# First stage with single k-steps between modulation pieces, and a projection with its short chunks between the long ones

## What is computed

```python
mod_x = silu(c) @ w_ada + b_ada          # 2048 -> 6 x 2048, also for c_ctx
sh1, s1, g1, sh2, s2, g2 = split(mod_x, 6)
h  = rmsnorm(x, norm1_w) * (1 + s1) + sh1     # and hc from ctx with the context's sh1, s1
p  = h @ w_in                                 # q, k, v | c_q (384) | c_kv (256) | k_rope (64)
q_mla = rmsnorm(c_q) @ w_uq
kv    = rmsnorm(c_kv) @ w_ukv
```

## Time and profile before

| | |
|---|---|
| median of 3 runs | 3177.64 us (3173.39 to 3178.29) |
| profiled execution | 3180.76 us, span 3178.9 us |
| PE busy | 2911.0 us, 92% of the span |
| DVE busy | 1804.0 us, 57% |
| ACT busy | 1191.1 us, 37% |
| mean granted TensorE clock | 0.96 of 2.4 GHz |

### The profile page before, as it was taken

How to read it: one execution, slowest core, us unless ns; L and a number is a source line. 1 busy time by engine, 2 the same in 40 slices (tenths; PEclk the granted TensorE clock), 3 DMA queues, 4 the chain that set the end, 5 groups by cost and what they waited for, 6 DMA issues and landing times.

```text
span 3178.9 us, 35028 instructions
## 1 busy us (share of the span) xinstructions
PE 2911.0 (92%) x13848; PEld 2378.0 (75%) x13848; DVE 1804.0 (57%) x2015; ACT 1191.1 (37%) x1134; POOL 165.0 (5%) x338
## 2 busy tenths in 40 slices
PE   5888895778999999999799999998879899999997
PEld 2587673467888888888587888887768788888886
DVE  1385776664555645555455557984754544555553
ACT  2232213433444434344344434333333343444332
POOL 0000005200000000000000100015300000000000
PEclk8999897999999999999889999999989999999999
DMA  8687875535456565546354876665236456555554
GB/s 333 245 293 259 304 255 185 179 132 192 164 172 206 174 210 186 184 162 206 96 199 169 269 224 215 223 201 167 60 120 207 150 164 207 199 189 193 169 174 134
DMA packets 347323, 617.34 MB, mean 194 GB/s; under 512 B 51232, under 2 KB 102064, under 8 KB 339776
## 3 DMA queue, kind: packets, MB, share of 16 engines
q1 hardware_dynamic: 310320, 582.69, 55.2%
q10 hardware_dynamic: 36880, 32.94, 3.1%
HBM read 586.57 MB, written 29.00 MB: 194 GB/s over the span
## 4 chain that ended last, share of the span: by engine, by line
PE 79%; DVE 11%; DMA 4%; ACT 3%; issue 2%; SPq 0%; POOL 0%; ACTq 0%; DVEq 0%; POOLq 0%
PE ps L306 21%; PE ps L307 21%; PE ps L308 21%; DVE w_lo L269 3%; PE ps L974 2%; PE ps L975 2%; PE ps L976 2%; DMA raw<-in_pack_ada 1%; DVE upd L2155 1%; PE ps L1199 1%; PE ps L587 1%; DVE w_lo L754 1%; DMA proj_q<-stg 1%; PE ps L2453 1%; PE ps L385 1%
## 5 line engine op out<-in xcount | busy, mean ns | idle before, releaser
L269 DVE TENSOR_TENSOR w_lo<-raw,w_hi 128x2048 fp32r<-128x2048 f32 (+3 forms) x428 | 892.0, 2094 | 703.7 <-ACT w_hi L262 702.4
L262 ACT ACTIVATE w_hi<-raw 128x2048 fp32r<-128x2048 f32 (+3 forms) x428 | 745.1, 1753 | 785.1 <-PE ps L308 728.0
L306 PE MATMUL ps<-w_hi,a_hi 128*128 128x512 f32 (+1 forms) x2272 | 892.2, 393 | 17.2 <-DVE a_lo L626 7.0
L308 PE MATMUL ps<-w_hi,a_lo 128*128 128x512 f32 (+1 forms) x2272 | 885.9, 390 | 0.0
L307 PE MATMUL ps<-w_lo,a_hi 128*128 128x512 f32 (+1 forms) x2272 | 885.6, 390 | 0.0
L306 PEld LDWEIGHTS ps<-w_hi,a_hi 128*128 128x128 f32 x2272 | 431.1, 190 | 109.8 <-DVE a_lo L626 8.7
L308 PEld LDWEIGHTS ps<-w_hi,a_lo 128*128 128x128 f32 x2272 | 430.8, 190 | 88.8
L307 PEld LDWEIGHTS ps<-w_lo,a_hi 128*128 128x128 f32 x2272 | 431.0, 190 | 85.6
L306 PE MATMUL ps<-w_hi,b_hi 128*128 128x512 f32 x864 | 339.0, 392 | 10.6 <-DVE w_lo L269 5.7
L308 PE MATMUL ps<-w_hi,b_lo 128*128 128x512 f32 x864 | 337.5, 391 | 0.0
L307 PE MATMUL ps<-w_lo,b_hi 128*128 128x512 f32 x864 | 337.4, 391 | 0.0
(11 more groups left out here) (319 smaller groups left out, 2788.3 us busy)
## 6 DMA issues: line engine op xcount, KB each, us to landing
raw<-in_hyb_w_in SPq DMA_DIRECT2D x96, 1024.0 KB, 5.3
raw<-in_sc_w_in SPq DMA_DIRECT2D x96, 1024.0 KB, 5.1
raw<-in_w_up SPq DMA_DIRECT2D x88, 1024.0 KB, 5.0
raw<-in_pack_ada SPq DMA_DIRECT2D x96, 512.0 KB, 6.2
raw<-in_w_down SPq DMA_DIRECT2D x48, 768.0 KB, 4.4
raw<-in_w_in SPq DMA_DIRECT2D x24, 1024.0 KB, 7.3
raw<-in_hyb_w_out SPq DMA_DIRECT2D x32, 768.0 KB, 4.5
raw<-in_sc_w_out SPq DMA_DIRECT2D x32, 768.0 KB, 4.4
```

The lines of the kernel that those rows point to most:

```text
L262: nc.scalar.activation(w_hi[s][:, 0:n_k, 0:ncols], raw[s][:, 0:n_k, 0:ncols], ACT.Copy).then_inc(sem("hi_done"), 1)
L269: nc.vector.tensor_tensor(w_lo[s][:, 0:n_k, 0:ncols], raw[s][:, 0:n_k, 0:ncols], w_hi[s][:, 0:n_k, 0:ncols].bitcast(F32), ALU.subtract).th ...
L306: nc.tensor.matmul(o, h, w_hi[s][:, k, 0:ncols], start=kt == 0, stop=False)
L308: last = nc.tensor.matmul(o, l, w_hi[s][:, k, 0:ncols], start=False, stop=kt == L.groups[-1][0] + L.groups[-1][1] - 1)
```

## The change

The k-steps of pieces 0 to 2 (12 matmuls each) are issued one at a time, after the modulation pieces 15 to 18, 20 to 23 and 27 to 30. ACT and DVE get a new order in the stage: the first quarter's `h_high` stand between the `z_copy`, `proj_hi` comes behind the forms of its quarter, `ada_copy` of a coming quarter is taken earlier. In the projection q0 goes ahead to 16 to 19, uk0 and uq0 are 20 and 21, K1 22 to 25, uk1 and uq1 26 and 27, q1 28 to 31, then uk2, uq2, uk3, uq3 (32 to 35) and V1 (36 to 39). The late units are spread anew, each total is issued one piece later, and the flips of the key latent stand before pieces 14 and 15 where they stood before 13 and 14.

```diff
-        LATE_AFTER = [0] * 4 + [1] * 4 + [2] * 4 + [4] * 4 + [2] * 4 + [1] * 4 + [2] * 4 + [5] * 4 + [2] * 4 + [5] * 4
+        LATE_AFTER = [0] * 4 + [1, 1, 2, 2] + [3, 3, 4, 4] + [5, 5, 4, 4] + [2] * 4 + [1, 1] + [3, 4, 4, 4] + [2, 1
+                      ] + [2] * 4 + [1, 1, 1, 2] + [4, 5, 4, 4]
...
-            dense_after = {10: 0, 16: 1, 24: 2, 30: 3}
+            dense_after = {10: 0, 16: 1, 24: 2, 28: 3}
...
         def ada_pe(pe):
+            steps = [(p, k) for p in range(3) for k in range(GROUP)]
+            step_after = dict(zip((15, 16, 17, 18, 20, 21, 22, 23, 27, 28, 29, 30), steps))
             for n in range(N_FIRST):
-                if n in (14, 21, 28):
-                    proj_piece(pe, (14, 21, 28).index(n))
                 ada_first(pe, n)
                 if n % RING == 0 and n:
                     ada_total(pe, n // RING - 1)
                 if 8 <= n < 8 + KT:
                     z_flip(pe, n - 8)
+                if n in step_after:
+                    p, k = step_after[n]
+                    proj_piece(pe, p, (k,))
...
+            z_copy(act, 0)
+            for quarter in range(4):
+                q = 4 * quarter
+                if quarter == 0:
+                    for j in range(1, 4):
+                        z_copy(act, j)
+                        h_high(act, j - 1)
+                    h_high(act, 3)
+                    proj_hi(act, 0)
+                    for j in range(4, 9):
+                        z_copy(act, j)
+                elif quarter == 1:
+                    for j in range(4, 8):
+                        h_high(act, j)
+                        if j < 7:
+                            z_copy(act, j + 5)
+                    proj_hi(act, 1)
+                    for j in range(12, KT):
+                        z_copy(act, j)
+                else:
+                    if quarter == 3:
+                        proj_hi(act, 3)
+                    for j in range(q, q + 4):
+                        h_high(act, j)
+                    if quarter == 2:
+                        proj_hi(act, 2)
...
+            forms(0, 3)
+            ada_copy(dve, 2)
+            forms(3, 4)
+            ada_out(dve, chain, 2)
+            proj_lo(dve, 0)
+            ada_copy(dve, 3)
+            ada_out(dve, chain, 3)
+            forms(4, 8)
+            ada_copy(dve, 4)
+            proj_lo(dve, 1)
+            ada_out(dve, chain, 4)
+            ada_copy(dve, 5)
+            ada_out(dve, chain, 5)
+            forms(8, 12)
+            proj_lo(dve, 2)
+            ada_copy(dve, 6)
+            ada_out(dve, chain, 6)
+            ada_copy(dve, 7)
+            ada_out(dve, chain, 7)
+            proj_lo(dve, 3)
+            forms(12, KT)
...
+        def up_pair(n):
+            return (("uk", W_UKV, n * CHUNK, CHUNK, True, PKV), ("uq", W_UQ, n * UQ_N, UQ_N, False, PQ))
...
-            *[("uk", W_UKV, n * CHUNK, CHUNK, True, PKV) for n in range(4)],
-            *[("uq", W_UQ, n * UQ_N, UQ_N, False, PQ) for n in range(4)],
-            ("in", W_IN, 0, CHUNK, False, PROJ_X), ("in", W_IN, OFF_K + CHUNK, CHUNK, True, PROJ),
-            ("in", W_IN, CHUNK, CHUNK, False, PROJ_X), ("in", W_IN, OFF_V + CHUNK, CHUNK, True, PROJ))
+            ("in", W_IN, 0, CHUNK, False, PROJ_X), *up_pair(0), ("in", W_IN, OFF_K + CHUNK, CHUNK, True, PROJ),
+            *up_pair(1), ("in", W_IN, CHUNK, CHUNK, False, PROJ_X), *up_pair(2), *up_pair(3),
+            ("in", W_IN, OFF_V + CHUNK, CHUNK, True, PROJ))
...
-        LAT_AT = {10: (0, 1), 11: (2,), 13: (3, 4), 14: (5, 6)}
+        LAT_AT = {10: (0, 1), 11: (2,), 14: (3, 4), 15: (5, 6)}
...
-            for M in late_ends(p - 1):
-                late_total(pe, M)
+                for M in late_ends(p - 2):
+                    late_total(pe, M)
```

More of the change, by code:

```diff
@@ L512, in ada_dve, with forms @@
             nc.vector.memset(sub02, LAMBDA_INIT).then_inc(sem("consts"), 1)
-            def quarter_of(q):
-                for j in range(4 * q, 4 * q + 4):
+            def forms(first, last):
+                for j in range(first, last):
                     h_form(dve, j)
-                    if j > 4 * q:
+                    if j > first:
                         h_low(dve, j - 1)
-                h_low(dve, 4 * q + 3)
+                h_low(dve, last - 1)
             ada_copy(dve, 0)
@@ L946, in proj_acts, with proj_piece @@
             return [(tile_of(a_hi), tile_of(a_lo)), (tile_of(b_hi), tile_of(b_lo))]
-        def proj_piece(pe, p):
+        def proj_piece(pe, p, steps=None):
             j, g = PIECES[p]
@@ L953, in proj_piece @@
             acts = proj_acts(kind)[0:2 if both else 1]
-            if p in LAT_AT:
-                lat_flip(pe, LAT_AT[p])
-            for M in late_ends(p - 1):
-                late_total(pe, M)
[L958 to L966, removed]
+            if steps is None or 0 in steps:
+                for M in late_ends(p - 2):
+                    late_total(pe, M)
+                if p in LAT_AT:
+                    lat_flip(pe, LAT_AT[p])
+                if g == 0:
+                    for c in range(ACC[j], ACC[j] + len(acts)):
+                        if c >= 3:
+                            pe.wait_ge(proj_free(c)[0], c // 3)
+                if j in (K0, QL):
+                    pe.wait_ge(sem("flip_lo"), 4 * (g + 1))
+                if kind in ("uk", "uq"):
+                    pe.wait_ge(sem("flip_lo"), LAT0 + 7)
+                pe.wait_ge(sem("lo_done"), p + 1)
             s = p % RING
-            for k in range(n_k):
+            for k in range(n_k) if steps is None else steps:
                 kt = kt0 + k
@@ L976, in proj_piece @@
                         last = nc.tensor.matmul(o, l, w_hi[s][:, k, 0:ncols], start=False, stop=kt == groups[-1][0] + groups[-1][1] - 1)
-            last.then_inc(sem("piece_used"), 1)
+            if k == n_k - 1:
+                last.then_inc(sem("piece_used"), 1)
         def proj_pe(pe):
@@ L981, in proj_pe @@
                 proj_piece(pe, p)
-            for M in late_ends(N_PROJ - 1):
-                late_total(pe, M)
+            for p in range(N_PROJ - 2, N_PROJ):
+                for M in late_ends(p):
+                    late_total(pe, M)
         put = region(B0, X0)
```

## The result

The changed kernel takes 3197.89 us (median of 4 runs, 3197.23 to 3200.79), the kernel before 3175.51 (4 runs, 3173.39 to 3178.29). The ratio is 1.0062 with a 95% interval of 1.005 to 1.0075: slower by some 20 us (22 by the medians), beyond the 6.4 us that a measurement can tell. The forecast was 3175.6 with a range of 3160 to 3190, so the time lies outside it.

What follows compares the result with a forecast made beforehand. PE was taken as the bound, with DVE close behind. 12 us won up to piece 4, 5 lost in pieces 4 to 15 and 5 lost in 16 to 39 made 2 won: 3175.6 us, range 3160 to 3190.

Steps and rivals of the forecast that it cites:

- The wait for `w_lo` of piece 2: First stage: PE idle from 110.8 until w_lo is ready at 117.4, 6.6 us.
- splitting the piece into k-steps takes nothing from this: First stage, piece 2: its first k-step needs all of w_lo, so the 6.6 us wait stays.
- the 1.5 us for the clock: First stage: taken off the 13.6 us won at piece 4 for a low clock after waits, leaving 12.
- the rival of the clock: Clock falls between first-stage k-steps, twelve at half speed: 3201 us; decides from three such steps on; chance 0.07.
- the split costs nothing: First stage: k-steps between modulation pieces cost nothing, as a stretch without them kept the full 2.4 GHz.
- 1.4 in two small ones: Pieces 4 to 15: two small PE waits, 1.4 us, besides 2.6 before piece 11's flip.
- The long wait before `lat_flip`: Before piece 14: PE waits for DVE's units, eviction, statistics and scaling of the key latent, 8.6 us, at least 8.1.
- this adds nothing: Pieces 16 to 39: ACT's w_hi of 24, 29 and 38 behind evictions cost nothing, PE being a piece ahead.
- the load terms, 3.4 at K1 and 1.9 at V1: Pieces 16 to 39: piece 22's load moves uk0's eviction from 38.0 to 41.4; the fifth slot adds 1.9 before uk3's.
- the rival of late loads: Late loads delay splits, units and evictions: 3188 us; decides once landings in pieces 8 to 24 exceed 7.3 by 2; chance 0.17.
- Hidden, at nothing: Edits priced at zero: piece 3's load sooner, earlier ada_copy, and each total one piece later.
- the gate (units 32, 40 and 64): Projection: these units, opening blocks 4, 5 and 8, wait for a PE total, delaying DVE before piece 14, K1, uq1.

Runs made afterwards that it cites:

- the best kernel: The changed kernel with evictions sooner, totals and late_out sooner, and the late units up to piece 15 as before the change: 3154.38 us, ratio 0.9928.

## Why the prediction was wrong

**First stage: right in mechanism, 3 us off.** 12 us won were forecast, 9.1 were measured, at the low bound of 9. The wait for `w_lo` of piece 2 was sized well (6.6, measured 6.97; its own terms, 107.9 + 5.7 + 1.9 + 2.3 - 110.8, make 7.0), and "splitting the piece into k-steps takes nothing from this" held. The term that was too small is the 1.5 us for the clock. Two stretches of the changed kernel, columns as in the earlier trace rows, are at half clock for most of their time.

```profile
89.80:94.40 4.60, 4.54 (x16) 3.35 (x20) 0.17 (x1) 0.00 (x0) 0.00 (x0) 0.63 0.66 269
120.40:125.20 4.80, 4.74 (x16) 3.54 (x20) 0.52 (x1) 0.00 (x0) 0.00 (x0) 0.60 0.59 188
```

The first is a k-step of piece 1: 4.6 us where I had 2.7, behind waits of 1.56 and 0.84 us. The second is the one after the wait of 6.97. Together they took 3.9 us more than two steps at full speed, where 1.5 were given: 2.4 of the 3 us. The other ten ran at full speed, so the rival of the clock (from three such steps on) did not come true. Nor is it the split that brings the clock down: with whole pieces it falls at the same two places (0.60 over 87.7 to 92.0 and over 118.3 to 123.0), and in the best kernel the k-step behind the first two waits ran at 1.00 (89.3 to 92.3). So "the split costs nothing" holds as far as these runs go. The Trainium skill's advice (TensorE: Matmul & The Clock Gate, HAM oscillation) to keep a tile's k-tiles together would give back at most the 3.2 us of the trace, and none of it in the time.

**Pieces 4 to 15: 5 lost forecast, 14.9 measured; the failed step is "1.4 in two small ones".** The long wait before `lat_flip` was there, with the releaser named and the size (8.6, measured 8.20), and so was the one before piece 11 (2.6, measured 3.56). Of the 1.4 in two small ones, 1.34 came before piece 10. Missing is the one of 7.07 before piece 12, for which nothing but the rest of the 1.4 was there. I asked when DVE would be ready for KL and did not follow ACT's queue: the store that empties KL's token side stands behind `lat_high`, that behind DVE's latent, that behind five units of a position, the last of which waits 2.90 us for PE. The run with the units as before (0.84 before piece 12) shows that their list causes it, the run with earlier totals (5.90) that the gate is the smaller part. It brought the clock down as well: 5.5 us over work and waits, 3.3 forecast; without the waits the stage ran at 1.00.

**Pieces 16 to 39: 5 lost forecast, 15.9 measured; the failed steps are "this adds nothing" and the load terms, 3.4 at K1 and 1.9 at V1.** The four places and their order were right: K1, uq1, V1, uk3, with evictions behind units. uq1 was met (5.2, measured 4.91). K1 came out at 13.75 for 9.2 and V1 at 18.34 for 13.7, 4.6 us more each.

At K1, counted from the end of V0, the eviction of uk0 ended at 47.2 where I had 41.4, 5.8 us later, and PE was through at 33.6 for 32.2. I had said that "ACT waits for the same evictions" but that PE has a piece ahead, so nothing is lost. PE has; DVE has not. After its eviction of V0, DVE's next instruction is a split whose `w_hi` ACT makes only once that eviction is done, so DVE stands for 2.46 us (290.35 above; the same at 394.92 and 425.36), and this delay goes into the next eviction. The rest, some 3.5 us, is loads: 5.32 for that of piece 22 with 1.6 for those of two late units, where I had given 3.4 in all.

At V1, counted from the end of q1, the eviction of uk3 ended at 39.6 where I had 34.7. The 2.4 for `w_hi` was in that sum. Missing are 3.6 us behind the eviction of uk2, where three loads of late units took 5.4 (2.11, 0.62 and 2.64) for the 1.9 that I had given, and 1.3 ahead of it, where two splits waited 1.52 and 0.76. So the rival of late loads is in it too: not by three splits of over 3 us (one was, 5.32), but by small ones on the one queue that sets the evictions. The loads themselves were not slow: those of 1 MB from 165 to 330 us took 7.4 us in the median, against 7.3 in the earlier trace rows.

That the eviction's place in the queue is the cause is shown by the run with sooner evictions: the 18.34 and 13.75 turned into 6.20 and 7.04, both for a split. What comes next there is the wait for a store on ACT's queue (8.28 and 8.12), which the prediction had only for uk3 and uq3.

**The gate of totals.** Under "Hidden, at nothing" stood "each total one piece later, since no block needs its buffer sooner except where named". That step costs much: undoing it, together with the sooner `late_out`, gave 26 us. Where I had named the gate (units 32, 40 and 64) the waits were there, and were priced: 8.20 and 4.91 of what that run took away were forecast. So the 26 us are not what the forecast missed by, but what this part of the change cost; I had kept it as free and added up what came of it elsewhere. The first unit of a block stands at the head of DVE's queue, and 48.9 us of DVE's time went into such waits. Which wait of PE each belongs to was not parted.

**The rivals.** None came true by itself. The slower outcome by the clock was the nearest in time (3201), but two steps fell where it asked for three, so that is chance. The one by late loads (3188) is in part in what came, but its sign, landings 2 us over 7.3, did not come. I had 24 in 100 for slower. Two terms, piece 12 and K1, were taken along one queue and are set by a chain over three.

**What stays open.** How much of the 26 us belongs to the totals and how much to `late_out`, and what the old order of chunks would give with all of the later edits, was not run. Why the stage after 499 us is 4.7 us shorter in the changed kernel (2697.1 for 2701.8) was not tried; the traces of the eleven runs above spread over 2698.2 to 2703.0 there, with nothing changed in it.

## What to carry to other kernels

An eviction placed at a fixed distance behind its chunk is safe only as long as PE has that distance of work; when short chunks are put ahead of a long one, shorten the distance with them, and look at what the eviction itself waits for (here a store), as that moves ahead with it. Where an engine runs a fixed order, ask of each wait what stands ahead of the releasing instruction in its queue, and then the same for that one, ACT's included; a busy share of 55% told nothing here. A reused buffer between two engines (total of block b before unit one of block b + 2) is a gate that delays all that stands behind it, so its position is to be planned like a deadline.

## What was unexpected of the hardware

The granted clock fell to 0.63 over 89.8 to 94.4 us, behind idle times of only 1.56 and 0.84 us with a modulation piece, a total and a flip around them, while in the kernel before the stretch from 80.5 to 92.7 kept 1.00. Behind the same two waits the best kernel kept 1.00 from 89.3 to 92.3, so they do not decide it alone. And with the waits of pieces 4 to 15 removed, 111.5 us of the same matmuls kept 1.00 throughout, at 0.87 of the DMA engines' time and 299 GB/s; that was more than the 273 GB/s of the stage with the waits, so the transfers were not at a limit there.
